# Triangular inverses of a hybrid decoder layer: 16x16 diagonal blocks on GpSimd, paired sub-block products at the two upper levels

## The reference

```python
def step(S, inp):
    r_t, w_t, k_t, v_t, kk_t, a_t = inp
    s_kk = jnp.einsum('bhvk,bhk->bhv', S, kk_t)
    S = (S * w_t[:, :, None, :]
         - s_kk[..., None] * (kk_t * a_t)[:, :, None, :]
         + v_t[..., None] * k_t[:, :, None, :])
    return S, jnp.einsum('bhvk,bhk->bhv', S, r_t)
...
_, y = lax.scan(step, S0, seq_inputs)
```

## Time and profile before

| | |
|---|---|
| median of 3 runs | 1758.3 us |
| profiled execution | 1760.37 us, its span 1758.6 us |
| busy: PE, DVE, ACT, POOL | 1676.8, 1358.4, 1058.7, 627.4 us |
| granted TensorE clock, mean | 0.972 |
| input products (until the first fox step) | 0 to 202.8 us |
| attention with the inversion of tiles 0 and 1 | 202.8 to 334.1 us |
| inversion of tiles 2 and 3 with the recurrence | 334.1 to 493.9 us |
| output projection, router; then the experts | from 493.9 us |

### The profile page before, as it was taken

The page is one execution under the profiler, slowest core; times in us unless marked ns, Lnnn a source line. Parts: engine busy times, 40 slices in busy tenths (PEclk is TensorE's granted clock), DMA queues, the critical chain, the costliest instruction groups (busy, mean ns, idle before and its releaser), DMA issues.

```text
span 1758.6 us, 24401 instructions
## 1 busy us (share of the span) xinstructions
PE 1676.8 (95%) x8420; PEld 1232.7 (70%) x8420; DVE 1358.4 (77%) x1174; ACT 1058.7 (60%) x942; POOL 627.4 (36%) x373
## 2 busy tenths in 40 slices
PE   6899899898999899999999999999999999999993
PEld 5587787688856576777777777777777777777772
DVE  4479745532426799999899989998999999999992
ACT  4334255322204577777777777777777777777772
POOL 6534221123232422334343344334433444343420
PEclk9999799999999899999999999999999999999996
DMA  5322000200115899999999999999999999999994
GB/s 174 110 72 72 1 1 1 96 1 1 49 34 192 321 329 380 391 375 376 369 382 376 381 363 380 381 381 368 377 384 377 375 375 380 377 374 374 381 344 127
DMA packets 136980, 466.11 MB, mean 265 GB/s; under 512 B 11959, under 2 KB 25437, under 8 KB 136861
## 3 DMA queue, kind: packets, MB, share of 16 engines
q1 hardware_dynamic: 127116, 436.31, 65.6%
q0 software_dynamic: 9664, 28.53, 6.9%
q10 hardware_dynamic: 144, 0.52, 0.1%
HBM read 443.15 MB, written 22.18 MB: 265 GB/s over the span
## 4 chain that ended last, share of the span: by engine, by line
PE 84%; DVE 7%; DMA 4%; issue 2%; POOL 2%; ACT 2%; SPq 0%; DVEq 0%; POOLq 0%; ACTq 0%
PE banks L1563 19%; PE banks L1565 19%; PE banks L1564 19%; PE banks L1508 3%; PE banks L1394 2%; PE banks L1404 2%; DMA slots<-in_expert_w_dram 2%; PE banks L1232 2%; PE banks L1233 2%; PE banks L1234 2%; PE banks L1572 2%; PE banks L1284 1%; PE banks L1558 1%; PE banks L1592 1%; PE banks L1411 1%
## 5 line engine op out<-in xcount | busy, mean ns | idle before, releaser
L1876 DVE TENSOR_TENSOR lo<-slots,hi 128x2048 fp32r<-128x2048 f32 x384 | 862.9, 2286 | 55.2 <-PE banks L1565 49.1
L1025 ACT CAST hi<-slots 128x2048 fp32r<-128x2048 f32 x384 | 734.1, 1912 | 241.8 <-PE banks L1565 131.0
L1563 PE MATMUL banks<-lo,x_hi 128*96 128x512 f32 x1024 | 408.1, 399 | 0.0
L1565 PE MATMUL banks<-hi,x_lo 128*96 128x512 f32 x1024 | 403.7, 394 | 0.0
L1564 PE MATMUL banks<-hi,x_hi 128*96 128x512 f32 x1024 | 402.7, 393 | 0.0
L829 POOL DMA_INDIRECT x_sum<-hT,idy x32 | 95.7, 2992 | 460.3 <-ACT hT L1110 446.7
L854 POOL COPY idx_all<-ovf_pair 96x2 int32 x28 | 161.3, 5760 | 158.6 <-DMA ovf_pair<-slot_tokens,ovf_col 158.6
L1565 PEld LDWEIGHTS banks<-hi,x_lo 128*96 128x96 f32 x1024 | 165.9, 162 | 72.4
L1564 PEld LDWEIGHTS banks<-hi,x_hi 128*96 128x96 f32 x1024 | 166.3, 162 | 67.5
L1563 PEld LDWEIGHTS banks<-lo,x_hi 128*96 128x96 f32 x1024 | 165.9, 162 | 66.8
L1563 PE MATMUL banks<-lo,a_hi 128*96 128x512 f32 x512 | 202.9, 396 | 5.5 <-DVE a_lo L2054 4.1
(11 more groups left out here) (375 smaller groups left out, 2129.5 us busy)
## 6 DMA issues: line engine op xcount, KB each, us to landing
slots<-in_expert_w_dram SPq DMA_DIRECT2D x384, 1024.0 KB, 10.7
slots<-in_w_in_dram SPq DMA_DIRECT2D x13, 1024.0 KB, 5.4
xs<-in_x_dram SPq DMA_DIRECT2D x8, 512.0 KB, 5.8
slots<-in_w_out_dram SPq DMA_DIRECT2D x2, 2048.0 KB, 8.5
x_sum<-xs SPq DMA_DIRECT2D x4, 512.0 KB, 8.7
h_rows<-slots SPq DMA_DIRECT2D x4, 512.0 KB, 2.7
xs<-x_sum SPq DMA_DIRECT2D x4, 512.0 KB, 6.8
x_sum<-xs POOLq DMA_DIRECT2D x3, 512.0 KB, 10.2
```

The lines of the kernel that those rows point to most:

```text
L1025: nc.scalar.copy(w_hi[n % HI][:, :, :], raw[r]).then_inc(hi_ready, 1)
L1563: nc.tensor.matmul(out, x_h, w_l, start=first, stop=False)
L1565: return nc.tensor.matmul(out, x_l, w_h, start=False, stop=last)
L1876: tensor_tensor(w_lo[n % LO][:, :, :], raw[n % RAW], w_hi[n % HI][:, :, :], ALU.subtract).then_inc(lo_ready, 1)
```

## The change

Levels 0 to 3 of all tiles are no longer done on TensorE, VectorE and GpSimd in the way above. All eight L stages now come in the first four fox steps; L of tiles 2 and 3 lies in the front half of hT. SyncE writes the 16x16 diagonal blocks of L to memory (16 DMAs of 16 partitions, 16 heads and tiles, 64 bytes each) and reads them back so that every partition holds two whole blocks. GpSimd inverts them there by back substitution, 15 times two instructions. SyncE writes the result out and brings it into XT, cleared before by GpSimd, with 8 DMAs. Fox steps 4 to 13 stand alone; the inversion of tiles 0 and 1 starts after step 13, and X0 waits for the last DMA. Level 4 is done as before. At levels 5 and 6 only the products that are not zero are done: for a pair of blocks lo and up of width 32 or 64, P is L[lo, up] times X[lo, lo] and XT[lo, up] gets the product of P and XT[up, up]; such a stage holds eight 32x32 products (level 5, all heads, one pair of blocks) or four 64x64 ones (level 6). They read Lm itself, which GpSimd copies next to the other tiles for tiles 2 and 3, and no mask is needed but that of level 4.

```diff
     assert NOVF + 2 <= E - 4
     KAPPA = 0.6065306597126334
     LEVELS = 7
+    LOW = 4
+    DB = 1 << LOW
...
+        def sub_blocks(lv, hf):
+
+            w = 1 << lv
+            if lv == LEVELS - 1:
+                return slice(0, w), slice(w, 2 * w), slice(4 * hf, 4 * hf + 4)
+            o = 2 * w * hf
+            return slice(o, o + w), slice(o + w, o + 2 * w), slice(0, H)
...
+        fox_stages = [("fox", i) for i in range(FOX_STEPS)]
+        rwkv_stages = between(fox_stages[:4], [("L", tt, g) for tt in range(NC) for g in range(2)])
+        rwkv_stages += fox_stages[4:FOX_ALONE] + between(fox_stages[FOX_ALONE:], inversion((0, 1)))
         rwkv_stages += between(inversion((2, 3)),
                                prepare(0) + [("U", 0), ("Yfrom", 0), ("state", 0), ("Y", 0)]
...
+            elif kind == "L":
+                put(st, 4 + nth_of["L"] % 4)
+                nth_of["L"] += 1
+            elif kind in ("X0", "P", "X", "XT") and tt < 2:
                 put(st, 4 + 2 * tt + nth_of[tt] % 2)
                 nth_of[tt] += 1
-            elif kind in ("L", "X0", "P", "X", "XT"):
+            elif kind in ("X0", "P", "X", "XT"):
                 put(st, 3 * (tt % 2) + nth_of[tt % 2] % 3)
                 nth_of[tt % 2] += 1
...
+            for pair in range(2):
+                sp.wait_ge(scm_ready, 2 * pair + 2)
+                for k in range(ND):
+                    at = slice(k * DB, (k + 1) * DB)
+                    sp.dma_start(diag_in[k, pair * 2 * H:(pair + 1) * 2 * H].rearrange("m r c -> r m c"),
+                                 L_pairs[pair].rearrange("p q h t -> p (q h) t")[at, :, at]).then_inc(diag_written, 16)
+            sp.wait_ge(diag_written, 16 * 2 * ND)
+            sp.dma_start(dblock.rearrange("p a r c -> p (a r c)"),
+                         diag_in.rearrange("k (m a) r c -> (k m) (a r c)", a=2)).then_inc(diag_read, 16)
+            sp.wait_ge(diag_inverted, 1)
+            sp.dma_start(diag_out.rearrange("k (m a) r c -> (k m) (a r c)", a=2),
+                         dinv.rearrange("p a r c -> p (a r c)")).then_inc(inverse_written, 16)
+            sp.wait_ge(xt_cleared, 1)
+            sp.wait_ge(inverse_written, 16)
+            for k in range(ND):
+                at = slice(k * DB, (k + 1) * DB)
+                sp.dma_start(XT.rearrange("p q h t -> p (q h) t")[at, :, at],
+                             diag_out[k].rearrange("m r c -> r m c")).then_inc(xt_in, 16)
             w_out_v = w_out[0].rearrange("(k p) f -> p k f", p=P)
...
+            filled(pool, "bonus")
+            pool.wait_ge(elem_done, JT)
+            step(nc.gpsimd.memset(dinv, 0.0))
+            select(dinv, [[0, 2], [1, DB], [-1, DB]], ALU.not_equal, 1.0, 0, 0)
+            nc.gpsimd.memset(XT.rearrange("p q h t -> p (q h t)"), 0.0).then_inc(xt_cleared, 1)
+            pool.wait_ge(diag_read, 16)
+            for s in range(DB - 1, 0, -1):
+                rest = dprod[:, 0:2 * s * (DB - s)].rearrange("p (a r c) -> p a r c", a=2, r=s)
+                shape = [P, 2, s, DB - s]
+                step(nc.gpsimd.tensor_tensor(rest, dblock[:, :, 0:s, s:s + 1].to_broadcast(shape),
+                                             dinv[:, :, s:s + 1, s:].to_broadcast(shape), ALU.mult))
+                step(nc.gpsimd.tensor_tensor(dinv[:, :, 0:s, s:], dinv[:, :, 0:s, s:], rest, ALU.subtract))
+            pool.sem_inc(diag_inverted, 1)
...
+                if kind == "X0" and st[2] == 1:
+                    pool.wait_ge(scm_ready, tt + 1)
+                    if tt >= 2:
+                        filled(pool, "P", tt - 2, LEVELS - 1, 1)
+                    nc.gpsimd.tensor_tensor(CT[:, tt % 2], Lm[tt], levmask[:, LOW, :].unsqueeze(1).to_broadcast([C, H, C]), ALU.mult)\
                         .then_inc(ct_ready, 1)
+                    if tt >= 2:
+                        nc.gpsimd.tensor_copy(L_near[tt], Lm[tt]).then_inc(l_moved, 1)
...
+                    if lv >= PAIRED:
+                        lo, up, of_heads = sub_blocks(lv, hf)
+                        if tt >= 2:
+                            pe.wait_ge(l_moved, tt - 1)
+                        for half in range(2):
+                            emptied(pe, "X", tt, lv - 1, half)
+                        for n, h in enumerate(range(of_heads.start, of_heads.stop)):
+                            ins = nc.tensor.matmul(packed(ps, of_heads, 1 << lv)[up, n, :], L_near[tt][lo, h, up], Xm[lo, q, h, lo],
+                                                   start=True, stop=True)
+                        end(ins, *st)
+                        continue
                     if hf == 0:
                         ncts += 1
                         pe.wait_ge(ct_ready, ncts)
...
                     ps = begin(*st)
                     emptied(pe, "P", tt, lv, hf)
-                    if lv > 1:
+                    if lv >= PAIRED:
+                        lo, up, of_heads = sub_blocks(lv, hf)
+                        for half in range(2):
+                            emptied(pe, "XT", tt, lv - 1, half)
+                        for n, h in enumerate(range(of_heads.start, of_heads.stop)):
+                            ins = nc.tensor.matmul(packed(ps, of_heads, 1 << lv)[lo, n, :], Pm[up, q, h, lo], XT[up, tt, h, up],
+                                                   start=True, stop=True)
+                        end(ins, *st)
+                        continue
+                    if lv > LOW:
                         emptied(pe, "XT", tt, lv - 1, hf)
                     for n in range(4):
                         h = 4 * hf + n
...
                                   ALU.mult).then_inc(free_of(st), 1)
                     emptied(dve, *st)
                     if g == 1:
                         dve.sem_inc(scm_ready, 1)
-                        step(tensor_tensor(XT[:, tt], Lm[:, q], levmask[:, 0, :].unsqueeze(1).to_broadcast([C, H, C]), ALU.mult))
-                        tensor_tensor(XT[:, tt], ident[:, :].unsqueeze(1).to_broadcast([C, H, C]), XT[:, tt],
-                                      ALU.subtract).then_inc(xt0_ready, 1)
                 elif kind == "XT":
                     lv, hf = st[2], st[3]
                     filled(dve, *st)
```

More of the change, by code:

```diff
@@ L130, in hymba_layer, with packed @@
         qkf = qk[:, :, :, :].rearrange("p a j t -> p (a j t)")
+        L_pairs = [m.rearrange("p (q h t) -> p q h t", q=2, h=H) for m in
+                   (region(slot_flat[4], JT * T, 2 * H * C), region(hT[:, :, :].rearrange("p k t -> p (k t)"), 0, 2 * H * C))]
+        Lm = [L_pairs[tt // 2][:, tt % 2] for tt in range(NC)]
+        L_near = [L_pairs[0][:, tt % 2] for tt in range(NC)]
+        def sub_blocks(lv, hf):
[4 more added lines that the diff above has]
+            return slice(o, o + w), slice(o + w, o + 2 * w), slice(0, H)
+        def packed(ps, heads, w):
+            return ps[:, 0:(heads.stop - heads.start) * w].rearrange("p (h c) -> p h c", c=w)
+        DW = 2 * DB * DB
+        dblock, dinv = (region(qkf, n * DW, DW).rearrange("p (a r c) -> p a r c", a=2, c=DB) for n in range(2))
+        dprod = region(qkf, 2 * DW, DW)
         fv2 = slot_flat[5]
@@ L330, in hymba_layer @@
         scm_ready = sem("scm_ready")
-        xt0_ready = sem("xt0_ready")
+        diag_written = sem("diag_written")
+        diag_read = sem("diag_read")
+        diag_inverted = sem("diag_inverted")
+        inverse_written = sem("inverse_written")
+        xt_cleared = sem("xt_cleared")
+        l_moved = sem("l_moved")
+        xt_in = sem("xt_in")
         ct_ready = sem("ct_ready")
@@ L439, in hymba_layer @@
         FOX_STEPS = len(units) + 4
+        FOX_ALONE = 13
         def inversion(pair):
-            st = [("L", tt, g) for tt in pair for g in range(2)]
-            st += [("X0", tt, hf) for tt in pair for hf in range(2)]
-            for lv in range(1, LEVELS):
+            st = [("X0", tt, hf) for tt in pair for hf in range(2)]
+            for lv in range(LOW, LEVELS):
                 st += [("P", tt, lv, hf) for tt in pair for hf in range(2)]
@@ L466, in between @@
             return st
-        rwkv_stages = between([("fox", i) for i in range(FOX_STEPS)], inversion((0, 1)))
+        fox_stages = [("fox", i) for i in range(FOX_STEPS)]
+        rwkv_stages = between(fox_stages[:4], [("L", tt, g) for tt in range(NC) for g in range(2)])
+        rwkv_stages += fox_stages[4:FOX_ALONE] + between(fox_stages[FOX_ALONE:], inversion((0, 1)))
         rwkv_stages += between(inversion((2, 3)),
@@ L1037, in _ @@
                     move(st, four_heads(Xm[:, q], st[2]), ps)
+                elif kind == "X" and st[2] == LEVELS - 2:
+                    lo, _, of_heads = sub_blocks(LEVELS - 1, st[3])
+                    move(st, Xm[lo, q, of_heads, lo], ps.rearrange("p (h t) -> p h t", h=4)[lo, :, lo])
                 elif kind == "X":
                     move(st, four_heads(Xm[:, q], st[3]), ps)
+                elif kind == "P" and st[2] >= PAIRED:
```

(21 more changed lines are left out.)

35 lines of the change are left out of this document (11 added, 24 removed).

## The result

The changed kernel takes 1736.0 us (median of 4 executions, 1734.5 to 1740.8) against 1757.5 us before on the same chip: ratio 0.9881, 95% interval 0.9859 to 0.9904. It is faster by 21 us. I had forecast 1714 us and a gain of 44; the sign is right, the range holds the time, and a little more than half of the gain is missing.

What follows compares the result with a forecast made beforehand. TensorE was taken to bound attention with the first inversion (gain 4 us) and the second inversion with the recurrence (gain 40); 1760.4 - 44 = 1716, less 2.1, gave 1714 us, range 1684 to 1745.

Steps and rivals of the forecast that it cites:

- the subtraction for B: Second inversion with the chunk recurrence, 159.8 us before: removals leave 101.4, added bank 6 waits make 119, a gain of 40.
- half clock after B's waits 5: Recurrence stretch: TensorE's half clock after the pair of first-XT waits would go, saving about 5 us.
- 18 us of waits on bank 6: Recurrence stretch: with thin stages between, waits for bank 6 to be emptied would add 18 us, bounds 8 and 28.
- Small products: Levels 5 and 6: at 35 ns a record, stages take 0.56 and 0.28 us, saving 17 us of TensorE in all.
- Rival (b): Levels 5 and 6: small products cost what full ones cost, 33 us more, giving 1747 us; chance 12%.
- The trip: Blocks through memory beside attention: a 36 us chain puts inverses in XT at about 257; TensorE waits 15 us.
- Stretch A: Attention with the first inversion: ends at 330 instead of 334.1, gaining only 4 us though losing 43 us of work.
- The waits that should go: TensorE's waits for the first XT, 12.0 us over both stretches, and for yT, 4.7 in the recurrence, would disappear.
- rival (c): Trip through memory is long: DMAs at upper bounds and GpSimd at 22 us put XT at 282, 1739 us; chance 13%.
- fall to 0.50 at X0: Sign in attention: TensorE's clock would fall to 0.50 at its 10 to 20 us idle before the first X0.
- in under 105 us: Sign against the forecast: the recurrence stretch ending in under 105 us would show the steps wrong.

Runs made afterwards that it cites:

- e3: Changed kernel with full products again at levels 5 and 6 and level masks on GpSimd, leaving only the trip through memory; 0.9786 of before.
- e11: Kernel before the change with only the small products at levels 5 and 6 added; 1.0017 of before.
- e9: Changed kernel, small products kept, with bank 6 stages going round banks 6, 2 and 5 and ScalarE's square root four stages later; 0.9691 of before.
- e7: Changed kernel with full products for tiles 2 and 3, bank 6 stages round banks 6, 2 and 5, and square root four stages later; 0.9680 of before.
- e1: Changed kernel with ScalarE's square root of the first two tiles' normalization four stages later; 0.9798 of before.
- e4: Changed kernel with the first three tiles' bank 6 stages going round banks 6, 2 and 5, two inversion banks each for tiles 2 and 3; 0.9769 of before.
- e10: e9 with four unread full products added in each small stage of tiles 2 and 3; 0.9724 of before.
- e2: Changed kernel with small products replaced by full ones of about equal length, off-diagonal blocks at levels 5 and 6 not computed; 0.9831 of before.
- e5: Changed kernel with four unread full products added in each small stage of tiles 2 and 3; executions of 1725, 1745, 1753 and 1758 us, no ratio.
- e6: Changed kernel with full products at levels 5 and 6 for tiles 2 and 3, small ones kept for tiles 0 and 1; 0.9776 of before.

## Why the prediction was wrong

The step that failed is the subtraction for B, in its term for the clock. I took "half clock after B's waits 5" away and added 18 us of waits on bank 6, and reckoned everything else at full-clock prices. B would have been 121 us between the cuts used here; it was 148.4.

- **Clock in B.** Forecast: 12.9 - 5 = 8 us lost. Measured: 41.5. That is 33.5 us, more than all that was missing. e3 shows that putting small products in the place of full ones makes the difference (3.7 lost with the same waits), e11 that it does so without the trip, and that after an idle the clock then does not come back for 43 us of work without a gap. e9 against e7 shows it with TensorE equally busy, with a fall that no idle precedes; e1, e4 and e9 lose less with fewer waits (32.7, 32.2, 16.8). The Trainium skill ("TensorE: Matmul & The Clock Gate", HAM oscillation) states the rule as one about idle gaps of TensorE. Idle gaps are not enough to account for e11's window of 28.00 busy us at 0.50 or for the fall in e9: here what the stages were made of mattered, not only whether one was running. Whether it is the small shape or the full work that is missing is less clear. e10 (small stages and filler, 0.96) and e2 (no small product in B, but as short, 0.77) speak for the missing full work; e5, filler with the waits, had 0.79 in its profiled execution.
- **Waits of bank 6.** Forecast 18 us, and 4.3 of before's waits left. Measured 14.3 us of waits in B, 8 less. But 7.1 of them are two idles that I had not named, ScalarE's square root ahead of the copy. The pieces of 0.7 to 0.8 us were as forecast.
- **Small products.** Level 5 alone 0.61 us for 0.56, level 6 0.61 for 0.28. For 32 stages about 6 us of gain less, half of it in B. The 35 ns came from products with 64 columns that accumulate in pairs; for 32x32 they hold (32 to 38 ns), for 64x64 not (67 to 76). Of a lone stage 0.15 to 0.19 us is the change to small products and back, if that is what the second stage of a pair saves; the prediction had allowed for up to 0.3. Rival (b), the price of a full product, is out.
- **The trip.** GpSimd 14.0 us (forecast 14.4, bounds 9 to 22) and the read 2.7 (3) were right. The DMAs were shorter: 5.0 for 7.5, 6.0 for 8, the store 2.1 for 3; the 8 us more that packets of twice the length would have cost did not show. TensorE was ready for X0 39 us after the start of the attention, as forecast, and waited 7.7 us, not 15.
- **Stretch A.** 3.7 us for a forecast of 4, which is luck: two errors cancel. Counted to the end of A that the prediction used, 1.7 us behind the cut, the chain was 7 us shorter (47.1 us from the start of attention to X0 for 54.2), and what follows X0 took 80.5 us instead of 72.6. In it the clock stayed at 0.50 for 17 us (247 to 264) at a loss of 8.5 us where I had allowed 5; that is about half of the difference, and the rest was not traced. Seven other profiles with the same instructions in A (e1, e4 to e7, e9, e10) have 120.1 to 124.5 us; this one, of the slowest execution, is the longest.
- **The waits that should go** (X0's 12.0 on VectorE and yT's 4.7) are gone.
- **The range.** That it holds 1736 is luck as well. The measured time lies next to rival (c) at 1739, but (c) was a long trip, and the trip was shorter than forecast; 1736 came about by the clock, for whose lasting loss the prediction had neither a term nor a rival.
- **Signs.** I had written that TensorE would fall to 0.50 at X0; it had been there since 200, through all the bare attention steps. B "in under 105 us" would have proved me wrong on the low side; I had no sign for the high side, and no rival with a lasting half clock. The trace of the kernel before had a hint of one: full products until 196.5, no wait over 0.33 us, then the 32 two-column products from 197.85, and in the midst of them, at about 200, the clock fell:

```profile
200.00:208.00 8.00, 8.00 (x46) 7.34 (x47) 1.79 (x4) 1.93 (x4) 0.13 (x1) 0.50 0.00 0
```

I had noted the "falling clock" and used the line only as the price of a narrow product.

The sum for B, from the forecast: 121 + 33.5 (clock) - 8 (waits) + 3 (small products) = 149.5, measured 148.4. That it closes so well owes something to chance, since the lost time is counted a little high.

Left open: which of the thin stages counts for how much (KAR and BR with 64 rows, transposes, small tiles), since only the small ones were changed; whether shape or the amount of full work decides; and why the same program keeps the clock in one execution and loses it in another (e5, e6).

## What to carry to other kernels

Work taken off TensorE saves its full-clock time only if what is left still holds the clock. Before pricing a change that replaces full products by small ones, look at the granted clock in a stretch where the thin stages already stand alone, and price one version at half clock throughout: here that version would have warned of the small products of levels 5 and 6 beside the recurrence. With the waits as they were, full ones were better by about 18 us (e6, 0.9776 for 0.9881); with both wait edits the two can't be told apart (e7 0.9680, e9 0.9691). And when cover gets thin, walk each emptying engine's queue for an instruction that waits on another engine; one square root cost two idles of over 3 us, and moving it by four stages took 15 us off the changed kernel (e1).

## What I had not expected of the hardware

- TensorE at 0.50 for 28 us while busy 28.00 of 28.00 us (e11), and in e9 the fall from 1.00 to 0.50 at 362.5, with no wait since 344.85.
- Executions of one program 33 us apart with the mean granted clock (e5: 1725.3 us at 0.964, 1758.4 at 0.943): 0.021 of 1740 us is 37 us, about the difference.
- Eight DMAs of 256 pieces of 64 bytes took SyncE's queue 4.9 and 3.7 us to issue, and the second batch had landed 5.0 us after its start; GpSimd's small dependent products cost 0.24 to 0.45 us for 30 to 128 elements a partition (two of them 0.76 and 0.94), about 0.08 us apart.
